# First weight half loaded between the second and third token tile; the first output unit's products regrouped to begin with two tiles and without low parts

## The reference

```python
h = jnp.concatenate([meta, x], axis=1)
u = rms_norm(h, norm_mix_g[l])          # x * rsqrt(mean(x^2) + eps) * g
z = u @ w_in[l] + b_in[l]               # 1024 x N_IN, the combined projection
a, gate = jnp.split(zc, 2, axis=-1)     # first 2048 columns of z
y = a * jax.nn.sigmoid(gate)            # input of the 31-tap convolution
```

## Time and profile before

| | |
|---|---|
| Time, median of 3 runs | 1666.99 us (1665.14 to 1667.73) |
| Span of the profiled execution, first to last instruction | 1658.8 us |
| Median less span: what lies around the span | 8.2 us |
| PE busy | 1594.7 us (96%) |
| PEld busy | 922.8 us (56%) |
| DVE, ACT, POOL busy | 653.5, 399.1, 427.2 us |
| Chain that ended last | PE 90%, DVE 3%, ACT 2%, POOL 2%, DMA 1% |
| DMA | 495 MB, mean 299 GB/s |

### The profile page before, as it was taken

The page is one execution under the profiler, slowest core; times in us unless marked ns, Lnnn a source line. Parts: engine busy times, 40 slices in busy tenths (PEclk is TensorE's granted clock), DMA queues, the critical chain, the costliest instruction groups (busy, mean ns, idle before and its releaser), DMA issues.

```text
span 1658.8 us, 38370 instructions
## 1 busy us (share of the span) xinstructions
PE 1594.7 (96%) x16168; PEld 922.8 (56%) x16168; DVE 653.5 (39%) x1222; ACT 399.1 (24%) x604; POOL 427.2 (26%) x465
## 2 busy tenths in 40 slices
PE   6999999998999999999999999999999999999992
PEld 6998987776888944344334434433443443344341
DVE  3699786214424352232223223222322322232237
ACT  4333123455312241121122112112211211221121
POOL 6334333344343442112111211211121121112114
PEclk9999999999999899999999999999999999999996
DMA  7563223221166449999999999999999999999995
GB/s 209 177 194 114 78 77 100 69 83 52 51 239 228 139 139 404 411 413 411 408 410 412 400 409 412 404 404 411 409 398 404 412 399 404 410 410 396 407 421 214
DMA packets 133886, 495.22 MB, mean 299 GB/s; under 512 B 17281, under 2 KB 76841, under 8 KB 84084
## 3 DMA queue, kind: packets, MB, share of 16 engines
q1 hardware_dynamic: 114452, 467.08, 71.9%
q0 software_dynamic: 8880, 16.54, 3.0%
q10 hardware_dynamic: 10512, 11.01, 2.0%
HBM read 476.32 MB, written 27.34 MB: 304 GB/s over the span
## 4 chain that ended last, share of the span: by engine, by line
PE 90%; DVE 3%; ACT 2%; POOL 2%; DMA 1%; issue 1%; SPq 0%; POOLq 0%; ACTq 0%; DVEq 0%
PE banks L1375 40%; PE banks L990 25%; PE banks L1424 20%; PE banks L1361 2%; DVE mix_lo L1678 1%; DMA stage<-in_w_in_dram 1%; PE banks L1339 1%; PE banks L1325 1%; ACT w_hi L724 0%; DMA y_last<-y_rows 0%; PE banks L1395 0%; POOL small L565 0%; DMA y_rows<-y_out,row_now 0%; ACT conv L858 0%; PE banks L1134 0%
## 5 line engine op out<-in xcount | busy, mean ns | idle before, releaser
L1375 PE MATMUL banks<-w_ring,xT 128*32 128x512 f32 x6144 | 671.0, 592 | 0.7 <-ACT xT L938 0.7
L1375 PEld LDWEIGHTS banks<-w_ring,xT 128*32 128x32 f32 x6144 | 198.7, 110 | 430.9 <-issue 422.3
L1424 PE MATMUL banks<-w_ring,actT 128*32 128x256 f32 x6144 | 344.0, 380 | 2.3 <-issue 2.3
L1424 PEld LDWEIGHTS banks<-w_ring,actT 128*32 128x32 f32 x6144 | 196.3, 110 | 146.2 <-issue 21.8
L1777 DVE TENSOR_TENSOR hid<-banks,bias 128x512 f32<-128x512 f32 x96 | 63.9, 665 | 477.2 <-PE banks L1375 475.7
L587 POOL TENSOR_TENSOR w_lo<-stage,w_hi 128x2048 fp32r<-128x2048 f32 x38 | 175.1, 4608 | 291.6 <-ACT w_hi L724 291.6
L990 PE MATMUL banks<-u_hi,w_hi 128*128 128x264 f32 (+1 forms) x544 | 183.8, 338 | 5.6 <-POOL w_lo L578 4.0
L990 PE MATMUL banks<-u_hi,w_lo 128*128 128x264 f32 (+1 forms) x544 | 181.7, 334 | 0.0
L990 PE MATMUL banks<-u_lo,w_hi 128*128 128x264 f32 (+1 forms) x544 | 181.1, 333 | 0.0
L961 ACT ACTIVATE bias<-banks 128x512 f32<-128x512 f32 x32 | 19.1, 597 | 559.9 <-PE banks L1395 559.9
L658 POOL COPY token_now<-token_of 96x1 int32 (+1 forms) x33 | 5.9, 180 | 565.0 <-PE banks L1361 561.4
(11 more groups left out here) (267 smaller groups left out, 1657.6 us busy)
## 6 DMA issues: line engine op xcount, KB each, us to landing
w_ring<-in_expert_w_dram SPq DMA_DIRECT2D x384, 1024.0 KB, 18.5
stage<-in_w_in_dram SPq DMA_DIRECT2D x20, 1024.0 KB, 5.2
y_rows<-empty_row ACTq DMA_DIRECT2D x8, 1280.0 KB, 5.3
stage<-in_w_in_dram SPq DMA_DIRECT2D x16, 512.0 KB, 5.4
y_in<-y_rows SPq DMA_DIRECT2D x4, 2048.0 KB, 22.1
stage<-in_conv_pw_w_dram SPq DMA_DIRECT2D x4, 1024.0 KB, 5.2
stage<-in_mlstm_out_w_dram SPq DMA_DIRECT2D x4, 1024.0 KB, 5.2
stage<-in_w_out_dram SPq DMA_DIRECT2D x4, 1024.0 KB, 5.5
```

What stands on the lines that cost most here:

```text
L1375: last = nc.tensor.matmul(banks[32 * g:32 * (g + 1), t].rearrange("p (c j) -> p c j", j=64), xT[:, k, 32 * t:32 * (t + 1)], units, start=k ...
L1424: last = nc.tensor.matmul(banks[32 * g:32 * (g + 1), 3 + t, 0:GRP], actT[:, t, k], w2_ring[k // 2][:, k % 2, GRP * g:GRP * (g + 1)], start ...
```

## The change

Four things move, in the first 32 us only.

1. SP issues half 0 of the first pair after tile 1 and ahead of tiles 2 and 3 (`load_first`).
2. ACT squares meta and tiles 0 and 1 only, copies parts 0 to 4 (`EARLY = 5`: meta, tile 0, tile 1), splits half 0, and only then squares tiles 2 and 3 and copies parts 5 to 8.
3. DVE makes low parts as it goes (`LOW_AFTER`): parts 0 to 2 after tile 1 is scaled, parts 3 and 4 after tile 2 is scaled, parts 5 to 8 after tile 3 is scaled.
4. PE transposes parts 0 to 4 and then does unit 0 in three groups of 16 matmuls, `first_terms`: high times high, as soon as `w_hi` of half 0 and `u_hi` of parts 0 to 4 are there; `u_lo` times `w_hi`, when the low parts 0 to 4 are there; then it transposes parts 5 and 6; `u_hi` times `w_lo`, when the low part of the weights is there; then it transposes parts 7 and 8. Unit 1 follows, behind the wait for all nine low parts and `vector_columns`. Part 8 takes bank 4 in place of bank 0 (`PART_BANK`), since unit 0 is summing in banks 0 and 1.

POOL's list is unchanged. The number of matmuls is unchanged.

```diff
+        PART_BANK = (0, 1, 2, 3, 4, 5, 6, 7, 4)
+        EARLY = 5
+        LOW_AFTER = ((), (), (0, 1, 2), (3, 4), (5, 6, 7, 8))
...
+            def load_first(s):
+                for part, off in enumerate((0, GATE_OFF)):
+                    sp.dma_start(stage[:, s, :, P * part:P * (part + 1)], win[:, :, off + P * s:off + P * (s + 1)]).then_inc(w_in_sem[s], 16)
...
             for i in range(TT):
                 sp.dma_start(x_sb[:, i], xt[i]).then_inc(x_in[i], 16)
-            load_glu(0, first=True)
+                if i == 1:
+                    load_first(0)
+            load_first(1)
...
-            for m, i in enumerate(ORDER):
+            def row_squares(m):
...
-            for j, (i, h) in enumerate(PARTS_OF_U):
-                if j == 4:
-                    split_hi(0, 0)
+            def high_part(j):
...
+            for m in range(3):
+                row_squares(m)
+            for j in range(EARLY):
+                high_part(j)
+            split_hi(0, 0)
+            for m in range(3, TT + 1):
+                row_squares(m)
+            for j in range(EARLY, 2 * TT + 1):
+                high_part(j)
             split_hi(0, 1)
...
-            for j, (i, h) in enumerate(PARTS_OF_U):
+            def x_part(j):
                 pe.wait_ge(scaled, (j + 1) // 2 + 1)
                 if j >= 8:
-                    pe.wait_ge(u_lo_made, j - 7)
+                    pe.wait_ge(u_lo_made, PART_BANK[j] + 1)
...
-            pe.wait_ge(u_lo_made, 2 * TT + 1)
+            def first_terms(n):
+                for c in range(2):
+                    for k in range(KT):
+                        hi, lo = weights(0, k, c)
+                        last = nc.tensor.matmul(banks[:, c, 0:HALF], lo if n == 2 else hi, (u_lo if n == 1 else u_hi)[:, k, halves[0]],
+                                                start=n == 0 and k == 0, stop=n == 2 and k == KT - 1)
+                if n == 2:
+                    last.then_inc(mm_done, 1)
+
+            def first_unit():
+                pe.wait_ge(u_lo_made, 2)
+                pe.wait_ge(u_hi_made, EARLY)
+                pe.wait_ge(w_hi_made[0], 1)
+                first_terms(0)
+                pe.wait_ge(u_lo_made, EARLY)
+                first_terms(1)
+                for j in (EARLY, EARLY + 1):
+                    x_part(j)
+                pe.wait_ge(w_lo_made[0], 1)
+                first_terms(2)
+                for j in range(EARLY + 2, 2 * TT + 1):
+                    x_part(j)
+
+            for j in range(EARLY):
+                x_part(j)
...
                 for h in range(2):
                     unit = 2 * ct + h
+                    if unit == 0:
+                        first_unit()
+                        continue
                     if unit == 1:
+                        pe.wait_ge(u_lo_made, 2 * TT + 1)
                         vector_columns()
...
             for n, i in enumerate(ORDER):
                 scaled_rows(n, i)
-            for j in range(2 * TT + 1):
-                low_part(j)
+                for j in LOW_AFTER[n]:
+                    low_part(j)
```

More of the change, by code:

```diff
@@ L382, in _, with load_pair, load_glu @@
         def _(sp):
-            def load_pair(n, source, first=False):
+            def load_pair(n, source):
                 for s in range(2):
-                    if not first:
-                        sp.wait_ge(w_lo_made[s], n)
+                    sp.wait_ge(w_lo_made[s], n)
                     sp.dma_start(stage[:, s], source(s)).then_inc(w_in_sem[s], 16)
-            def load_glu(n, first=False):
+            def load_first(s):
+                for part, off in enumerate((0, GATE_OFF)):
+                    sp.dma_start(stage[:, s, :, P * part:P * (part + 1)], win[:, :, off + P * s:off + P * (s + 1)]).then_inc(w_in_sem[s], 16)
+            def load_glu(n):
                 for s in range(2):
-                    if not first:
-                        sp.wait_ge(w_lo_made[s], n)
+                    sp.wait_ge(w_lo_made[s], n)
                     for part, off in enumerate((0, GATE_OFF)):
@@ L733, in _ @@
                 nc.scalar.activation(square_out[0:n], src, ACT.Square, accum_out=square_sum[0:n, i:i + 1]).then_inc(squared, 1)
[L735 to L737 removed]
+            def high_part(j):
+                i, h = PARTS_OF_U[j]
                 act.wait_ge(u_transposed, j + 1)
[L739 to L740 removed]
+                dst, src = (u_hi[:, 4 * h:4 * h + 4, META + P * i:META + P * (i + 1)], banks[:, PART_BANK[j]].rearrange("p (k t) -> p k t", t=P)) \
+                    if i < TT else (u_hi[:, :, 0:META], banks[:, PART_BANK[j], 0:KT * META].rearrange("p (k t) -> p k t", t=META))
                 nc.scalar.activation(dst, src, ACT.Copy).then_inc(u_hi_made, 1)
+            for m in range(3):
[7 more added lines that the diff above has]
+                high_part(j)
             split_hi(0, 1)
@@ L1016, in _ @@
                         col = P * (4 * h + k)
-                        last = nc.tensor.transpose(banks[:, j % 8, P * k:P * (k + 1)], x_sb[:, i, col:col + P], ident)
+                        last = nc.tensor.transpose(banks[:, PART_BANK[j], P * k:P * (k + 1)], x_sb[:, i, col:col + P], ident)
                 else:
                     for k in range(KT):
-                        last = nc.tensor.transpose(banks[:, j % 8, META * k:META * (k + 1)], meta_sb[:, P * k:P * (k + 1)],
+                        last = nc.tensor.transpose(banks[:, PART_BANK[j], META * k:META * (k + 1)], meta_sb[:, P * k:P * (k + 1)],
                                                    ident[0:META, 0:META])
                 last.then_inc(u_transposed, 1)
-            pe.wait_ge(u_lo_made, 2 * TT + 1)
+            def first_terms(n):
[21 more added lines that the diff above has]
+                x_part(j)
             def vector_columns():
```

9 lines of the change are left out of this document (6 added, 3 removed).

## The result

The changed kernel takes 1670.52 us (median of 20 runs, 1666.07 to 1674.65), the kernel before 1667.62 us in the same comparison (20 runs, 1664.44 to 1669.99). The ratio is 1.0016, with a 95% interval of 1.0009 to 1.0024: +2.7 us, 1.5 to 4.0. That is a small loss, inside the band that was called no change, and the time is inside the predicted range.

The account below looks back on a forecast made before the run. PE, almost always busy once begun, was taken as the bound, so the front's change passes to the end, measured at unit 1's start. Sum: span 1658.8 + 1.7 + 8.2 = 1668.7 us, range 1665.5 to 1672.0.

Parts of the forecast that it names:

- part 2: ACT's squares of tiles 2 and 3 behind the splitting: two roots precede POOL's `w_lo`, ending 26.1, 4.0 us later.
- part 1: SP's weight half 0 ahead of tiles 2 and 3: `w_hi` ready at 17.4, not 17.5, gain 0.1 us.
- part 3: DVE's new order: low parts 3 and 4 behind tile 2's scaling, done at 22.1; tile 3 scaled behind them.
- part 4: PE's three groups from 17.4, 22.1 and 27.6, clock rising at 27.5, nine-part wait bare; unit 1 at 33.0, +1.7 us.
- rival 1: Clock up from PE's second group, then a wait for `w_lo` to 26.1; unit 1 at 31.5, +0.2 us; chance 0.27.
- Rival 2: Clock low until well into unit 1, since only products raise it; unit 1 at 35.5, +6.6 us overall; chance 0.13.
- Rival 3: The change does what it says: products fill idle PE time, gain of more than 3.3 us; chance 0.04.
- Rival 4: Weight half 1 late, its 0.8 slack used up, 1 to 2 us lost at unit 2: about +3; chance 0.08.
- the cases: Whole-kernel times forecast for the possible outcomes: 1667.2, 1668.7, 1670 and 1673.6 us.
- the 1.3: Whole-kernel time: the 1.3 us by which single runs stand off their median, used for the range.

Follow-up runs that it names:

- the second profile: The changed kernel run again without an edit, in a second comparison: 1669.55 us against 1668.8 for the kernel before, ratio 0.9998.
- the earlier low parts: Changed kernel with DVE's low parts 3 and 4 ahead of tile 2's scaling; profiled, no ratio given, unit 1 at 31.34.
- the regrouping alone: Kernel before with only PE's unit 0 products regrouped in three, all other engines' lists unchanged: 1667.32 us against 1668.8, ratio 0.9989.

## Why the prediction was right, and where it was not

**The price, part 2 (held).** `w_lo` was to run 21.55 to 26.1, and it ran 21.24 to 25.79. That the moved squares cause it is shown by putting them back: the low part ends at 22.15 and unit 1 starts 1.9 to 2.7 us earlier (29.46 against 31.36 and 32.11; SP's order is undone in it too, which by itself gained nothing).

**The gain, part 1 (held).** 0.1 us for the early load; measured 0.12 against before, 0.2 with only SP's order undone.

**DVE, part 3 (held).** Low parts 3 and 4 done at 21.79 (forecast 22.1), tile 3 blocked for 5.17 us and hidden. It ended at 26.88 (27.4), and PE came to it at 28.66 (29.6), or 27.93 in the second profile: 1.8 or 1.1 us to spare, where the sum had 2.2. Both ways round were seen: POOL first by 0.07 us makes DVE 5.55, DVE first by 0.19 us makes POOL 5.51, where alone they take 1.28 and 4.55. The Trainium skill, SBUF — State Buffer, section "SBUF: two separate sides", calls this an exclusive lock that the first starter keeps for its whole instruction, and these rows agree with it.

**PE, part 4 (mechanism held, the clock's time did not).** First group 17.47 (17.4), second 21.84 (22.1), nine-part wait bare (1.57 before the vectors), unit 1 at 32.11 and 31.36 where I had 33.0. The term that was off is the rise of the clock, put at 27.5 from one row of before (5.3 us after the first product): it came near 26 in one profile, before 21.86 in another, and near 24 with the earlier low parts (second group 3.21). My forecast of unit 1 and rival 1's, 33.0 and 31.5, lay on both sides of the first measurement, which is a little nearer to rival 1's, and the second was rival 1's. The time to expect of the clock can't be read from one row.

**What was missing.** I let the clock stay up once it had risen, and named a granted clock of 0.50 in unit 1 as a sign against me. It came in the first profile, right behind what stood in my own list, the bare wait, and added 1.5 us there. That the wait brings the fall is argued from the count above. Two errors that partly cancel, unit 1 0.9 us earlier than forecast and 1.5 us lost behind it, left the sum near the truth (1.7 forecast, 2.3 at the sigmoid of this profile), and that is luck. Measured were +2.7 us, 1.5 to 4.0, in one comparison, and no difference in the other. **Rival 2** was right that the clock can have the last word on the wrong side, but not on how: transposes did bring it up. In the regrouping alone the first group takes 2.19 right behind 28 transposes that end at 17.60, and no products had come before. (Its 35.5 for unit 1 also has 0.3 more than the terms that it names, 33.1 + 1.3 + 0.77.) The Trainium skill, TensorE: Matmul & The Clock Gate, section "Part 4: PE-mode transpose", says that they don't count as activity (it gives times of bf16 ones only); that group, like the 421 and 272 ns of the earlier trace rows, disagrees.

**Rival 3** (faster than before) was given 0.04 for the changed kernel on good grounds: `w_lo` ends at 25.8, and third group, transposes and the rest must follow it. The regrouping itself does what it says: alone, it ends unit 0 at 24.65 and not 30.7, 6 us earlier. The change spent it. **Rival 4** did not come: half 1's low part ended at 36.85, and no wait for it is in the trace.

**Around the span.** I added 8.2 us, the median less the profiled span. That was wrong: in runs of which both are known, the time is 1.8 above the span (1668.59 and 1666.8 for the kernel before, 1671.03 and 1669.3 for SP's order undone). The first profile of before, 1658.8, was thus an execution of about 1660.6 us, 3.8 below the fastest of the 20 timed ones (1664.44), and its loop is the short one, 10 us less. The sum of 1668.7 came out right since the 8.2 carried me from that execution to the median. The range's ends, 1665.5 and 1672.0, are also a little wider than the cases and the 1.3 give (1667.2 - 1.3 = 1665.9, 1670 + 1.3 = 1671.3); rival 2's 1673.6 lies outside them.

## What to carry to other kernels

When work is pulled forward on one engine, follow what is pushed back on the others: here two squares of 1.25 us on ACT, moved behind a split, put two reciprocal roots ahead of a 4.55 us instruction on POOL, and the gain on PE was gone. Look for the smallest form of a change, here the order of products on PE alone, and then for the small thing that is late next (a load of a few bias rows behind four big ones), before reordering the rest. A wait of a microsecond or two directly in front of a long run of products may cost more than its length: in four of nine profiles the clock fell behind it. Where it costs nothing, let something useful stand there or move the wait to where work is queued.

## What the runs showed of the hardware

- The granted clock fell to 0.50 behind PE waits of only 1.57 to 2.26 us, in some executions and not in others: for about 3.5 us in the changed kernel, 6.5 in the regrouping alone.
- The column of the granted clock can mislead at the start: it has 1.00 for 17 to 21 us of the changed kernel, while the first group there takes 3.86 for 16 products, 0.22 apart, the lower level.
- With twelve small loads on ACT's queue, 1 MB on SP's queue landed at 21.2 us and not at 15.5 (one profile).
- The same kernel has medians of 1658.8 to 1668.8 us in five comparisons, and of 1658.8 and 1668.4 on one chip at two times. The experts' loop takes 967 or 977 us between the same two blocks, and nothing between: more than most changes of the front are worth.
